# Two weight pairs loaded a stage early, two products moved from GpSimd to VectorE, and key projections respaced, in a two-layer hybrid decoder step

## What is computed

```python
ada = silu(c) @ w_ada + b_ada                      # 48 columns of 128: shifts, scales, gates
h = x * (1 + scale1) + shift1
gq, gk, gv, gg, glr, lx, lgate, dq, dkv, kr = split(h @ w_in)
o_gla = rms_norm(gla(q, k, v, logf)) * silu(gg)    # chunked linear attention with a state
o_lru = gelu(lgate) * rg_lru(conv(lx))             # the recurrence and its last product
o_mla = latent attention, 8 heads (prompt: causal over 1024 keys; samples: 8192 cached keys each)
x = LN(alpha * x + gate1 * (concat(o_gla, o_lru, o_mla) @ w_out))
x = LN(alpha * x + gate2 * swiglu_ffn(x * (1 + scale2) + shift2))
```

## Time and profile before

| | us |
|---|---|
| median of 3 runs | 3480.62 |
| lowest and highest of them | 3478.95, 3488.60 |
| the profiled execution, its own time | 3485.3 |
| its span, first to last instruction | 3483.5 |
| TensorE busy in the span | 3255.1 (93%) |
| VectorE busy | 2326.5 (67%) |
| ScalarE busy | 1587.2 (46%) |
| GpSimd busy | 202.9 (6%) |
| mean granted TensorE clock | 0.966 of full |

### The profile page before, as it was taken

One profiled execution on the slowest core, in us unless ns is written; L12 is line 12 of the kernel. 1 busy time (PEld: TensorE's weight loads), 2 busy tenths in 40 slices (PEclk: granted clock), 3 DMA queues, 4 the chain that ended last, 5 costly groups with the idle time before them and its releaser, 6 DMA issues. The chain is left out here.

```text
span 3483.5 us, 61376 instructions
## 1 busy us (share of the span) xinstructions
PE 3255.1 (93%) x23676; PEld 2738.1 (79%) x23676; DVE 2326.5 (67%) x4390; ACT 1587.2 (46%) x3159; POOL 202.9 (6%) x254
## 2 busy tenths in 40 slices
PE   6988898998999999999989889989989999999997
PEld 4875566776998998999978655667769899899997
DVE  5254665444488889888844456644446888888878
ACT  5343554444255454444344445634433554544432
POOL 0020111110000000000001111011100000000000
PEclk9998999998999999999989889999989999999998
DMA  7026102443033332222121340044421333322231
GB/s 272 27 93 230 66 1 105 164 157 106 16 106 96 95 101 80 90 87 86 52 109 31 137 142 1 1 163 165 158 49 52 94 98 96 94 87 83 91 106 57
DMA packets 158149, 334.72 MB, mean 96 GB/s; under 512 B 18556, under 2 KB 85406, under 8 KB 146471
## 3 DMA queue, kind: packets, MB, share of 16 engines
q1 hardware_dynamic: 146342, 246.91, 22.2%
q0 software_dynamic: 11520, 83.89, 6.8%
HBM read 315.32 MB, written 15.43 MB: 95 GB/s over the span
## 5 line engine op out<-in xcount | busy, mean ns | idle before, releaser
L2494 ACT CAST w_ffn_hi<-w_ffn 128x512 fp32r<-128x512 f32 x616 | 371.3, 618 | 259.4 <-DVE w_ffn L2676 128.0
L445 PE MATMUL psum<-h_lo,w_ffn_hi 128*128 128x256 f32 (+1 forms) x1408 | 406.6, 289 | 0.0
L2688 DVE TENSOR_TENSOR w_ffn_lo<-w_ffn,w_ffn_hi 128x1024 fp32r<-128x1024 f32 (+1 forms) x366 | 383.0, 1047 | 11.8 <-ACT w_ffn_hi L2494 11.7
L444 PE MATMUL psum<-h_forms_hi,w_ffn_hi 128*128 128x288 f32 x1232 | 364.1, 296 | 3.4 <-DVE w_ffn_lo L2688 3.4
L446 PE MATMUL psum<-h_forms_hi,w_ffn_lo 128*128 128x288 f32 x1232 | 363.7, 295 | 0.0
L444 PE MATMUL psum<-h_hi,w_ffn_hi 128*128 128x256 f32 x1232 | 348.6, 283 | 10.9 <-DVE w_ffn_lo L2688 9.1
L444 PE MATMUL psum<-ffn_act_hi,w_down_hi 128*128 128x288 f32 (+1 forms) x992 | 332.3, 335 | 21.1 <-DVE w_down_lo L2694 6.5
L446 PE MATMUL psum<-h_hi,w_ffn_lo 128*128 128x256 f32 x1232 | 346.8, 281 | 0.0
L446 PE MATMUL psum<-ffn_act_hi,w_down_lo 128*128 128x288 f32 (+1 forms) x992 | 326.6, 329 | 0.0
L445 PE MATMUL psum<-ffn_act_lo,w_down_hi 128*128 128x288 f32 (+1 forms) x992 | 325.9, 328 | 0.0
L430 DVE SCALAR_TENSOR_TENSOR xT<-psum,adaT,xT 128x512 f32<-128x512 f32 (+2 forms) x320 | 191.1, 609 | 130.4 <-PE psum L446 127.0
(11 more groups left out here) (450 smaller groups left out, 7624.8 us busy)
## 6 DMA issues: line engine op xcount, KB each, us to landing
w_ffn<-in_w_gu SPq DMA_DIRECT2D x352, 256.0 KB, 2.6
w_ada_pair<-in_w_ada SPq DMA_DIRECT2D x40, 1024.0 KB, 6.1
w_down<-in_w_down SPq DMA_DIRECT2D x192, 192.0 KB, 2.4
residual_kept<-xT SPq DMA_DIRECT2D x2, 4352.0 KB, 19.2
xT<-residual_kept SPq DMA_DIRECT2D x2, 4352.0 KB, 14.2
w_ada_first<-in_w_ada SPq DMA_DIRECT2D x4, 2048.0 KB, 22.2
w_out<-in_w_out SPq DMA_DIRECT2D x16, 512.0 KB, 7.3
w_in_T<-in_w_in_T SPq DMA_DIRECT2D x12, 512.0 KB, 4.4
```

The costliest lines, as they stand in the source:

```text
L444: pe.matmul(o, wh, xh, start=first, stop=False)
L445: pe.matmul(o, wh, xl, start=False, stop=False)
L2494: act.copy(WGH[:, (j + 1) % NR].bitcast(F32R), WGR[:, m % 2, i]).then_inc(s_wh, 1)
L2688: dve.tensor_tensor(WGL[:, m % 2, i:i + n].bitcast(F32R), WGR[:, m % 2, i:i + n], WGH[:, r:r + n], ALU.subtract).then_inc(s_wl, n)
```

## The change

1. The two products of L1109 leave GpSimd. VectorE does them, one behind `states` in step 2 and one in step 3 (`MIXED_AT`).
2. The first two pairs (`NPA = 2`) are loaded by SP in `stage_in`: the first when `s_lf` is 2, into the place of `LI`/`LV`, the second when `s_h` is 2, into the place of `LR`. SP waits for both (`s_fa`) before it ends the stage. In `stage_gla` SP begins with pairs 2 and 3.
3. Each later step of pairs is regrouped: one pair more in step 1 and one fewer towards the end. In step 1 the first pair comes ahead of `cumulate(2)`.
4. In `stage_mla_prompt` the projections of the next head pair are spread out: no longer in ten iterations on end (5 to 14), but with gaps, and the two of keys are three iterations apart. The last may fall into the first iteration of the next head pair.
5. In the same stage ScalarE reads a projection ahead of `scale(i - 1)` in iterations after the fourth.

```diff
-        NWA = 4
+        NWA, NPA = 4, 2
         WAN = [at(f"w_ada_pair_{i}", o, [P, 2, KD, P]) for i, o in enumerate(
-            (o_ht + 4 * T * 4, o_ht + 4 * T * 4 + 8 * KD * P, o_xt + 2 * T * 4, o_xt + 2 * T * 4 + 8 * KD * P))]
+            (o_xt + 4 * T * 4, o_xt + 2 * T * 4, o_ht + 4 * T * 4, o_ht + 4 * T * 4 + 8 * KD * P))]
...
+        def ada_pairs():
+            return range(M_G1 // 2 if layer[0] == DEPTH - 1 else 0, ADA_PAIRS)
+        def ada_slab(eng, q, p):
+            return eng.dma_start(WAN[q % NWA], of("w_ada", ada_row(2 * p))[2 * p:2 * p + 2].rearrange("m p k n -> p m k n"))
...
-            pe.wait_ge(s_aw[q % NWA], 16 * (q // NWA + 1))
+            if q >= NPA:
+                pe.wait_ge(s_aw[q % NWA], 16 * (q // NWA + (q % NWA >= NPA)))
...
# stage_in, SP
                     sp.dma_start(of("conv_out"), CVO).then_inc(s_out, 16)
+                    sp.wait_ge(s_lf, 2)
+                    ada_slab(sp, 0, ada_pairs()[0]).then_inc(s_fa, 16)
                     sp.wait_ge(s_hn, 1)
                     sp.dma_start(of("lru_out"), HN).then_inc(s_out, 16)
+                    sp.wait_ge(s_h, 2)
+                    ada_slab(sp, 1, ada_pairs()[1]).then_inc(s_fa, 16)
                     sp.wait_ge(s_out, 32)
                     sp.wait_ge(s_p, 48)
+                    sp.wait_ge(s_fa, 16 * NPA)
...
# stage_gla
-        ADA_PER_STEP = {24: (1, 2, 3, 3, 3, 3, 3, 3, 2, 1), 16: (1, 2, 2, 2, 2, 2, 2, 2, 1, 0)}
+        ADA_PER_STEP = {24: (2, 3, 3, 3, 3, 3, 3, 2, 1, 1), 16: (2, 2, 2, 2, 2, 2, 2, 1, 1, 0)}
+        MIXED_AT = (2, 3)
...
-                    ada_load(sp, pairs[:2], s_aw, s_aa)
+                    ada_load(sp, pairs, s_aw, s_aa, NPA, NWA)
                     sp.dma_start(SSC, of("gla_state")).then_inc(s_si, 16)
-                    ada_load(sp, pairs, s_aw, s_aa, 2)
+                    ada_load(sp, pairs, s_aw, s_aa, NWA, len(pairs))
...
                     pool.memset(SBD, 0.0).then_inc(s_z, 1)
-                    for c in range(2):
-                        pool.tensor_tensor(HT[:, 2 + c], LG[:, c], XC[:, c], ALU.mult).then_inc(s_mx, 1)
                     pool.wait_ge(s_mx, 2)
...
                         if s <= NBLK:
+                            for q in todo[:1] if s == 1 else ():
+                                pair(q)
                             if s + 1 < NBLK:
                                 cumulate(s + 1)
-                            for q in todo[:1]:
+                            for q in todo[:1] if s > 1 else ():
                                 pair(q)
                             attend(s - 1)
...
                             mask(s - 1)
                             states(s - 1)
+                        if s in MIXED_AT:
+                            c = MIXED_AT.index(s)
+                            dve.tensor_tensor(HT[:, 2 + c], LG[:, c], XC[:, c], ALU.mult).then_inc(s_mx, 1)
...
# stage_mla_prompt
-            for hp in range(1, HP):
-                for j in range(NPJ):
-                    pj_at.setdefault((hp - 1) * PER + 5 + j, []).append((hp, j))
+            SPREAD = {hp: (5, 8, 9, 10, 11, 12, 13, 14, 15, 16) if hp == 1 else (1, 4, 5, 8, 9, 10, 12, 13, 14, 15)
+                      for hp in range(1, HP)}
+            for hp, at_items in SPREAD.items():
+                for j, x in enumerate(at_items):
+                    pj_at.setdefault((hp - 1) * PER + x, []).append((hp, j))
...
# ScalarE, behind the exponentials of item i
+                        for hp, j in pj_at.get(i, []) if i > 4 else ():
+                            read(hp * NPJ + j)
                         if i:
                             scale(i - 1)
                         for blk in v_at.get(i, ()):
                             if blk % 2 == 0:
                                 v_kept(blk)
-                        for hp, j in pj_at.get(i, []):
+                        for hp, j in pj_at.get(i, []) if i <= 4 else ():
                             read(hp * NPJ + j)
```

More of the change, by code:

```diff
@@ L489, in ada_row, with ada_load @@
             return None if m < M_G1 else DEPTH - 1 - layer[0]
-        def ada_load(eng, pairs, s_aw, s_aa, done=0):
-            for q, p in list(enumerate(pairs))[done:]:
+        def ada_pairs():
+            return range(M_G1 // 2 if layer[0] == DEPTH - 1 else 0, ADA_PAIRS)
+        def ada_slab(eng, q, p):
+            return eng.dma_start(WAN[q % NWA], of("w_ada", ada_row(2 * p))[2 * p:2 * p + 2].rearrange("m p k n -> p m k n"))
+        def ada_load(eng, pairs, s_aw, s_aa, q0, q1):
+            for q in range(q0, q1):
                 if q >= NWA:
                     eng.wait_ge(s_aa, q - NWA + 1)
-                eng.dma_start(WAN[q % NWA], of("w_ada", ada_row(2 * p))[2 * p:2 * p + 2].rearrange(
-                    "m p k n -> p m k n")).then_inc(s_aw[q % NWA], 16)
+                ada_slab(eng, q, pairs[q]).then_inc(s_aw[q % NWA], 16)
         def ada_turn(pe, p):
@@ L600, in stage_in @@
             s_wb = [sem(f"w_in_B_{k}_in") for k in range(KD)]
+            s_fa = sem("first_pairs_in")
             s_wa, s_wt, s_p = sem("w_in_A_in"), [sem(f"w_in_T_{i}_in") for i in range(3)], sem("params_in")
@@ L1071, in stage_gla @@
             s_az = sem("ada_bank_zero")
-            pairs = range(M_G1 // 2 if layer[0] == DEPTH - 1 else 0, ADA_PAIRS)
+            pairs = ada_pairs()
             PARTS = [(0, 4), (4, 7), (7, NBLK)]
```

## The result

The changed kernel takes 3428.2 us (median of 4 runs, 3426.2 to 3431.0), against 3479.8 us of the kernel before in the same job. The ratio is 0.985, 95% interval 0.983 to 0.987. Its profiled span is 3429.2 us, 54.3 less than before. Timed again later, it took 3427.4 us in five runs, ratio 0.985 (0.984 to 0.986).

The account below looks back on a forecast made before the run. TensorE's in-order list was taken as the bound, so idle time removed from it counts: 10.0 - 0.8 (linear attention, stage ends) + 18.6 + 2.0 (prompt attention, its clock) = 29.8 us off 3480.6, giving 3450.8 us; range 3432 to 3466.

Parts of the forecast that it names:

- Part 1: Linear attention start: GpSimd's products hold VectorE's L1327, stalling TensorE; moving them gains 4.4 + 1.7 us per layer.
- The 1.7 us per layer of slow rows behind the stall: Linear attention: low clock right behind TensorE's 6.76 us wait, taken as gone, 1.7 us per layer (bounds 0 and 1.7).
- rival A: Low clock in the middle of the linear attention goes as well: 19 us more gained, 3432 us; chance 0.13.
- if the low stretches change their length by tens of us: Sign, stated beforehand, that the prediction is wrong: low-clock stretches lengthen or shorten by tens of us.
- Part 2: End of `stage_in`: the second early load makes SP's new wait late by 0 to 0.8 us per layer, taken as 0.4.
- The rival of a load late by 6.9 us: End of `stage_in`: second load takes the longest 12.3 us, 6.9 us late per layer; a case within B.
- Part 3: Linear attention: first pair inside the stall gains 1.05 us per layer; new ScalarE waits cost 1.2 and 0.6 us.
- the 1.5 and 1.0 us that the forecast gave back at the stage's end: Linear attention: a pair leaves the place behind layer 0's last `attend` (1.5 us) and layer 1's step 8 (1.0).
- Part 4: Prompt attention: respaced projections and earlier reads remove key, query and latent waits, 9.3 us per layer, 18.6 in both.
- B: Prompt attention: earlier reads block ScalarE, or a second load lands late; 12 to 14 us given back, 3464 us; chance 0.12.
- C: Linear attention: the hold was not GpSimd's, L1327 stays at 5.56 us, 3461 us remain; chance 0.05.
- D: Linear attention: new waits spread the low clock, some 58 us lost in both layers, 3509 us; chance 0.03.

Follow-up runs that it names:

- the filled hold: The kernel before, with 20 extra unread TensorE products in the 6.76 us wait ahead of the third cumulative sum: 3473.0 us, ratio 0.9982.
- The part alone: The kernel before with only the prompt attention's edits (projections respaced, reads ahead of scalings): 3453.3 us, ratio 0.9915.
- second profile of after: The unmodified changed kernel, profiled and timed again beside a filled version: 3427.4 us, median of 5 runs.
- the run with the reads behind: The changed kernel with ScalarE's projection reads behind its scalings again, projections in their new places: 3432.2 us, ratio 0.9855.
- the filled waits: The kernel before with extra unread TensorE products in its long early wait, or in two later waits for ScalarE's copies: 3473.0 and 3472.6 us.

## Why the prediction was wrong

**Part 1, right in the wait, wrong in the clock: this is the step that failed.** The hold was GpSimd's, 4.4 us per layer went (5.56 to 1.17, and `cumulate(2)` 4.39 us earlier), L1135 has 0.70 at full clock, and the moved products cost nothing visible (1.29 us each, GpSimd's memset done at 269.9). The 1.7 us per layer of slow rows behind the stall is the term that was mis-sized. I had counted only the clock that I could see right behind the stall, and left the stretches of the earlier trace rows to rival A with a chance of 0.13. Over the first 60 us of the stage, clocks of 0.80 and 0.72 mean at most (0.20 + 0.28) x 60 = 28.8 us of full-speed work lost in the profile of before; 0.86 and 0.94 mean 12.0 in the first profile of after, and none in its second. Not all of that is won, since TensorE stands idle in a part of the low clock, and other low stretches came later in the stage. What was won is the busy time above: 10.8 us in the first profile and 18.5 in the second, where the sum had 3.4. The prediction had named this as a sign of being wrong, "if the low stretches change their length by tens of us", and in layer 1 the 26 us went. Rival A said 19 more, 3432 us; with it the prediction would have come out 4 us too high. It is near in the number by luck in part: the clock gave 7.4 us beyond the sum in one profile and 15.1 in the other, and idle time that A does not speak of made up the rest.

The reasoning that failed is the one against A: "a stretch that is busy in the record and slow all the same speaks against an easy use of it", and "they bring new waits of 1 to 2 us, so the busy share is hardly greater". Both facts are true, 247.5 to 263 us of after shows them again. But the kernel with only the pairs changed had the same hold, about the same busy time, and in its profile not the stretches. What the Trainium skill ("TensorE: Matmul & The Clock Gate", Part 1) says, that activity releases the clock, is borne out by the filled hold, where L1122 went from 1.22 to 0.59; no run here ties a later stretch to one gap.

**Part 2, right.** The second load was issued at 228.50, behind L667. Between ScalarE's last Gelu and the next stage lay 1.37 us in layer 0 and 1.81 in layer 1, against 1.04 and 1.33 before: 0.33 and 0.48 late, forecast 0.4. The rival of a load late by 6.9 us didn't come.

**Part 3, right in the size of the new wait, wrong in its sign.** The wait for ScalarE's copy is 1.30 us and stands in both layers (forecast 1.2 in layer 0, 0.6 in layer 1, as an addition). But it stands in place of two that the first steps of before had in each layer, the 1.20 us of the earlier trace rows and, in step 3, this one:

```profile
262.07 0.61 PE L500 MATMUL psum<-consts,ada_rows 128*128 128x9 f32 x4 [0.88 <-ACT ada_rows L515]
```

So 0.8 us per layer went where 1.2 and 0.6 were to be added, and the 1.5 and 1.0 us that the forecast gave back at the stage's end do not show as idle time either. That is the greater part of the 6 to 8 us of idle time won beyond the forecast. (In layer 0 the regrouping puts one pair more into step 1 and one into step 2, and takes them from steps 8 and 9; in layer 1 it is one, from step 8 to step 1.) Alone, pairs and loads made 12 us. By the clocks of its profile up to (0.11 + 0.22) x 60 = 20 us less is lost than in that of before.

**Part 4, right.** 6.4 + 1.5 + 1.3 = 9.2 us of waits per layer went, forecast 9.3. The part alone brought 25 us, forecast 20.6: in its profile the prompt attention was 12.3 and 12.1 us shorter, of which TensorE's idle time is 9.8 and 9.5 and its busy time, the clock's part, 2.5 and 2.6, forecast 1.0. In the changed kernel's layer 0 only 7.6 us came out, because the query weights landed 8.3 us after issue instead of 6.1 and TensorE waited 3.2 us. This wait was 1.6 us in its second profile, and 3.7 to 4.6 in four other kernels. I had not looked at how near that load was to being late: in layer 1 of the kernel before it was late already, by 2.3 us. Why it lands later is open.

**The rest** of the program, where nothing but the two early loads was changed, was 6.7 us shorter in the first profile of after and 0.4 us shorter in the second; that is the spread of an execution.

**The books.** Profile against profile, 54.4 us: linear attention 25.1 (forecast 10.0), prompt attention 22.6 (20.6), the rest 6.7 (-0.8). In the second profile of after, 58 us: 31.4, 26.2 and 0.4. Of the 22 us that the forecast missed, the linear attention has 15 in the first and 21 in the second: 7.4 and 15.1 by the clock, 7.7 and 6.4 by idle time. Why the clock stays up in one execution and not in another is open.

**Rivals.** B: ScalarE's reads cost nothing that shows; the run with the reads behind was not faster. C fell. D did not come.

## What to carry to other kernels

Price the low clock of the whole stage, not only the slow rows right behind the stall: (1 - granted clock) times the length of the stretch is the most that can be won, less where TensorE waits in it, and here the pairs, the products and the filled waits each won a part alone. Such a term belongs in the sum with a wide range of its own; in the linear attention it was about as large as all the idle time won. One profile is one draw of it, so take the mean granted clocks of all runs of a kernel too: they told the two kernels apart where single profiles contradicted each other, though they too overstate the time. Ask of a new wait also which old one it takes the place of. And where VectorE's short operations suddenly take 2.5 us, look for what GpSimd reads at that time.

## What the hardware showed unexpectedly

- A one-input GpSimd copy of 128x1088 (1.1 us) holds VectorE's two-input operations (2.76 us for four instead of 1.17) as the two-input product (2.5 us) does (5.56); a GpSimd memset of 128x2048 (1.8 us) doesn't.
- The clock stayed at its lower level for 16 us (247.5 to 263 us of after, mean 0.51) with TensorE's row full from end to end, and for 26 us in the kernel before; the same instructions behind the same waits ran at the full clock in another execution. In one kernel it was low for 30.5 us (mean 0.51) behind waits of only 0.60 and 0.49 us.
- 20 products that nobody reads, put into a wait of 6.8 us, took 8.8 us in one layer and 10.3 in the other and delayed the stage by 1.7 and 3.4 us, and the kernel still became 6 us faster (ratio 0.9982, interval below 1).
- Over the last 20 us of the linear attention the clock rose from 0.74 and 0.79 to 1.00 and 0.94, and the stage was not shorter (93.9 and 78.2 us against 93.0 and 78.0), while TensorE still waited for VectorE there: a low clock need not cost anything where another engine sets the pace.
